# A transformer step on one core: the mixer in two token passes, with the first expert gathers of tile 0 inside it, and GpSimd making one-hot factors

## What is computed

```python
def mixer_and_peer(x, h, o_mla, o_dil, lw):
    y = gate_a * (o_mla @ lw['w_branch_mla']) + gate_b * (o_dil @ lw['w_branch_dil'])  # gates: sigmoid(h @ w_gate)
    x = x + gt1 * (y @ lw['w_out'])
    h2 = modulate(x, lw['norm_ffn_g'], sh2, sc2)          # rms norm, scale, shift
    return x + gt2 * peer(h2, ...)

def peer(hx, w_pq, sub_keys, expert_u, expert_v):
    q = (hx @ w_pq).reshape(n, 8, 2, 128)
    s = einsum('nhpc,hpkc->nhpk', q, sub_keys)            # 8 heads x 2 axes x 128 keys
    top_s, top_i = top_k(s, 16)
    cand = top_s[:, :, 0, :, None] + top_s[:, :, 1, None, :]
    best_s, best = top_k(cand.reshape(n, 8, 256), 16)
    eidx = i1 * 128 + i2                                  # the two keys of each best pair
    g = softmax(best_s)
    a = gelu(einsum('nd,nhkd->nhk', hx, expert_u[eidx])) * g
    return einsum('nhk,nhkd->nd', a, expert_v[eidx])
```

## Time and profile before

| | |
|---|---|
| median of three runs | 4351.54 us (4319.0 to 4370.52) |
| profiled execution | 4370.86 us |
| its span, first to last instruction | 4369.1 us |
| busy: PE, DVE, ACT, POOL | 3802.1, 2723.7, 1199.4, 859.8 us |
| mean granted TensorE clock | 0.913 |

### The profile page before, as it was taken

How to read it: one execution, slowest core, us unless ns; L and a number is a source line. 1 busy time by engine, 2 the same in 40 slices (tenths; PEclk the granted TensorE clock), 3 DMA queues, 4 the chain that set the end, 5 groups by cost and what they waited for, 6 DMA issues and landing times.

```text
span 4369.1 us, 43255 instructions
## 1 busy us (share of the span) xinstructions
PE 3802.1 (87%) x14474; PEld 2490.1 (57%) x14474; DVE 2723.7 (62%) x6374; ACT 1199.4 (27%) x3244; POOL 859.8 (20%) x718
## 2 busy tenths in 40 slices
PE   8798899999981899967997677799999999899896
PEld 7575377888970788953453444344454444445443
DVE  2764562533534111258999987767779676967876
ACT  2564432322332111122222567421111111111111
POOL 0000000001000000003333223333333333344332
PEclk8898998995985899988999888899999999999997
DMA  4001102203116111237888879999999999999997
GB/s 158 7 1 42 29 37 80 81 20 119 51 40 208 55 41 36 100 108 282 323 327 318 314 302 376 399 417 409 410 399 378 414 412 387 384 409 412 387 354 279
DMA packets 255851, 1016.29 MB, mean 233 GB/s; under 512 B 28650, under 2 KB 103810, under 8 KB 170642
## 3 DMA queue, kind: packets, MB, share of 16 engines
q0 software_dynamic: 101520, 723.10, 41.9%
q1 hardware_dynamic: 131218, 280.65, 17.4%
q10 hardware_dynamic: 22896, 9.80, 0.8%
HBM read 964.22 MB, written 49.25 MB: 232 GB/s over the span
## 4 chain that ended last, share of the span: by engine, by line
PE 27%; DVE 15%; DMA 11%; issue 2%; ACT 2%; SPq 0%; POOL 0%; ACTq 0%; DVEq 0%
PE banks L2488 9%; PE banks L2474 9%; DMA ff_room<-in_v 7%; PE banks L2463 4%; DVE ff_rows L2137 4%; PE banks L2411 2%; DVE ff_acc L2103 2%; DMA gates_dram<-ff_room 2%; PE banks L2356 1%; DMA ff_rows<-in_uv,pk_expert 1%; DVE pk_eq L1793 1%; DVE pk_axes L1798 1%; DVE mx_x L2163 1%; PE banks L2435 1%; DVE pk_besti L1772 1%
## 5 line engine op out<-in xcount | busy, mean ns | idle before, releaser
L2035 POOL DMA_INDIRECT ff_rows<-in_uv,pk_expert x640 | 803.0, 1255 | 1519.2 <-DVE ff_acc L2103 831.8
L2137 DVE CUSTOM_DVE_ANT_0 ff_rows<-ff_rows,ff_h_row 128x1024 f32<-128x1024 f32 x648 | 766.6, 1220 | 45.3 <-DMA ff_rows<-in_uv,pk_expert 43.4
L2488 PE MATMUL banks<-ff_room,mx_x 128*128 128x512 f32 x1536 | 702.3, 608 | 57.9 <-DVE mx_x L2178 31.2
L2474 PE MATMUL banks<-mx_x,ff_room 128*128 128x384 f32 x2048 | 685.7, 488 | 12.2 <-ACT mx_x L2321 12.2
L2463 PE MATMUL banks<-ff_rows,o_mla_tops 128*128 128x512 f32 x904 | 446.5, 643 | 144.5 <-ACT o_mla_tops L2231 140.8
L2474 PEld LDWEIGHTS banks<-mx_x,ff_room 128*128 128x128 f32 x2048 | 390.3, 191 | 313.0 <-issue 77.3
L2488 PEld LDWEIGHTS banks<-ff_room,mx_x 128*128 128x128 f32 x1536 | 297.3, 195 | 418.9 <-issue 357.8
L2103 DVE SCALAR_TENSOR_TENSOR ff_acc<-ff_rows,ff_a,ff_acc 128x1024 f32<-128x1024 f32 x388 | 498.6, 1285 | 7.2
L2463 PEld LDWEIGHTS banks<-ff_rows,o_mla_tops 128*128 128x128 f32 x904 | 179.1, 206 | 361.8 <-issue 198.5
L177 PE MATMUL banks<-d_w_high,h_high 128*128 128x512 f32 (+1 forms) x648 | 274.3, 423 | 21.9 <-DVE d_w_low L184 21.0
L2219 ACT ACTIVATE ff_gelu<-ff_dots 128x2 f32<-128x2 f32 x324 | 65.7, 203 | 824.9 <-DVE ff_dots L2137 824.7
(11 more groups left out here) (391 smaller groups left out, 5660.3 us busy)
## 6 DMA issues: line engine op xcount, KB each, us to landing
ff_room<-in_uT SPq DMA_DIRECT2D x128, 512.0 KB, 14.4
ff_room<-in_v SPq DMA_DIRECT2D x128, 512.0 KB, 20.6
gates_dram<-ff_room SPq DMA_DIRECT2D x6, 4096.0 KB, 16.8
mx_x<-gates_dram SPq DMA_DIRECT2D x128, 192.0 KB, 17.2
d_w<-in_w_dil POOLq DMA_DIRECT2D x9, 2048.0 KB, 8.3
d_w<-in_w_ada POOLq DMA_DIRECT2D x32, 512.0 KB, 4.7
ff_room<-in_w_pq SPq DMA_DIRECT2D x32, 512.0 KB, 4.5
ff_rows<-in_uv,pk_expert POOLq DMA_INDIRECT x640, 10.8
```

Of the source, the lines that this page charges most:

```text
L2035: pool.indirect_dma_start(out=rows[r][:, :], out_offset=None, in_=IN["uv"][:, :], in_offset=bass.IndirectOffsetOnAxis(ap=at, axis=0))\
L2137: ins = dve.tensor_tensor_reduce(rows[r][:, 0:D], rows[r][:, 0:D], h_row[i % 2][:], 1.0, 0.0, ALU.mult, ALU.add, dots[:, B % RB, j:j + 1])
L2474: ins = pe.matmul(SD[:, 0:ND], u[e % 4][:, k, :], hd[:, k, :], start=(k == 0), stop=(k == KD - 1))
L2488: ins = pe.matmul(Y[j][:, half], ad[e % 2][:, j * P:(j + 1) * P], v[e % 4][:, half_rows[half]], start=(e == 0), stop=(e == NK - 1))
```

## The change

**stage_mix in two passes.** Pass 0 takes the first 256 tokens (`EARLY` tiles 0 and 1) through gates, output, residual and norm; pass 1 takes the other 776 in two chunks of 388. A unit is now one branch and one gate (`side`), 16 in pass 0 and 32 in pass 1, counted by `u` (by `z` from pass 1's start). All weight tiles are loaded and split twice. After pass 1's second unit (`ROUTER_AT`) come the queries, keys, top 16 and picks of tiles 0 and 1's router that stood in the next stage's prologue. Then 30 of tile 0's 64 batches (`MIX_BATCHES`) run inside pass 1: one per unit from `z` = 5 to 30 but for 16 and 28, then one per second output unit. They have two slots of two rows (`RB` = 2), and DVE does their dot products and their sums.

**stage_ffn.** Tile 0 has 34 batches left, so the dense loop begins at batch 98 instead of 128. `HOT0` is 58, with three quads per batch (`HOTS`), so 32 batches. POOL makes all first factors, behind the gathers of two batches later; ACT makes the second factors of every third quad (`by_act`), DVE those of the other two. There are two `stage` buffers; the second lies in four of the ten row buffers, and so batches 56 to 95 have three slots (`FEW`) instead of five. `ON_VEC` has 10 batches instead of 15. Rows of `h` go to memory from SP.

```diff
+EARLY, MIX_BATCHES = 2, 30
...
+    PASSES = [[(0, NE)], [(NE, NE + CB), (NE + CB, TOK)]]
+    SUBS = [(p, m, side, i) for p in range(2) for m in range(KD) for side in range(2) for i in range(len(PASSES[p]))]
...
+    ROUTER_AT = 1
+    BATCH_AT = [z for z in range(5, 31) if z not in (16, 28)] + list(range(33, 48, 2))
...
+            @block.gpsimd
+            def _(pool):
+                pool.wait_ge(s["half_tile"], 1)
+                for b in range(NB):
+                    for j in range(G):
+                        r = b % RB * G + j
+                        if b >= RB:
+                            pool.wait_ge(s["rsum"], (b - RB) * G + j + 1)
+                        at = c.expert0[:, b * G + j:b * G + j + 1]
+                        pool.indirect_dma_start(out=ring[:, r, :], out_offset=None, in_=IN["uv"][:, :],
...
+                def gated(u):
+                    p, m, side, i = SUBS[u]
+                    c0, c1 = PASSES[p][i]
...
+                    if u >= 3:
+                        pe.wait_ge(s["y"], u - 2)
+                    src = c.o_dilT if side else c.o_mlaT
+                    for k in range(KO):
+                        pe.matmul(out, wb[b % 2][:, side * KO + k, :], src[:, k, c0:c1], start=(k == 0), stop=(k == KO - 1))
+                    pe.wait_ge(s["w_lo"], n + 1)
+                    for k in range(KD):
+                        ins = product3(pe, gate, w_parts(n, k), [t[:, k, c0:c1] for t in h_parts], k == 0, k == KD - 1)
...
+                for u in range(S1, len(SUBS)):
+                    gated(u)
+                    if u == S1 + ROUTER_AT:
...
+                        queries(0)
+                        for hp in range(HP):
+                            if hp + 1 < HP:
+                                queries(hp + 1)
+                            scores(hp)
...
+                def weights(b):
+                    act.wait_ge(s["dot"], b + 1)
+                    act.activation(act_of[:, b % RB], dots[:, b % RB], ACT.Gelu).then_inc(s["gelu"], 1)
...
+                for z in range(len(SUBS) - S1):
+                    sums_due(z)
+                    mixed(S1 + z)
+                    for n in made_after(S1 + z):
+                        w_low(dve, n)
...
+                    if 2 <= z <= 4:
+                        picks(z)
+                    dots_due(z)
...
-    batches = [(i, b) for i in range(NS) for b in range(TAILB if i == TAIL else PER)]
+    batches = [(i, b) for i in range(NS) for b in range(0 if i else MIX_BATCHES, TAILB if i == TAIL else PER)]
...
-    PICK0, HOT0, HOTS = HP * LATE_PER + 3, HP * LATE_PER + 13, 2
+    PICK0, HOT0, HOTS = HP * LATE_PER + 3, HP * LATE_PER + 10, 3
...
+    by_act = lambda q: q % 3 == 1
+    FEW, FEW_AT, MANY_AT = 3, HOT0 - 2, HOT0 + QUADS // HOTS + 6
...
-        stage = part(0, NK * GBLK).rearrange("p (a n) -> p a n", n=GBLK)
+        second = ring[:, FEW * G:FEW * G + 4].rearrange("p r f -> p (r f)")
+        stage = [t.rearrange("p (a n) -> p a n", n=GBLK) for t in (part(0, NK * GBLK), second)]
...
+                    for q in quads_at(B - 2):
+                        pool.wait_ge(s["p_copy"], q // (P // 4) + 1)
+                        if q >= RQ:
+                            pool.wait_ge(s["hot_mm"], q - RQ + 1)
+                        for k in range(4):
+                            at = 4 * q + k
+                            ins = pool.tensor_scalar(hot1[q % RQ][:, k], c.iota[:], pick(0, at), pick(2, at),
+                                                     ALU.is_equal, ALU.mult)
+                        ins.then_inc(s["hot1"], 1)
...
-                        for k in range(4):
-                            at = 4 * q + k
-                            ins = dve.tensor_scalar(hot1[q % RQ][:, k], c.iota[:], pick(0, at), pick(2, at),
-                                                    ALU.is_equal, ALU.mult)
-                        ins.then_inc(s["hot1"], 1)
-                        if q % 2:
-                            continue
...
-                                act.wait_ge(s["g_out"], 16 * (q // BQ))
+                                act.wait_ge(g_out[q // BQ % 2], 16 * (q // BQ // 2))
```

More of the change, by code:

```diff
@@ L11 @@
 import concourse.bass as bass
+import math
 import numpy as np
@@ L1563, in stage_mix @@
         ts = sb("ts", [P, KD, NSA])
[L1564 to L1568, removed]
+        dots, act_of, a = (sb(t, [P, RB, G]) for t in ("dots", "gelu", "a"))
@@ new lines, in stage_mix @@
+        pk = Picks(c, ctx, [0], "px_", [c.expert0], [c.gate0],
+                   [c.x_normed[:, at:at + PH // 2, 0:NE] for at in (0, PH // 2)])
+        acc, h_row = c.acc0, c.o_mlaT[:, :, 0:NE]
+        s = {n: c.sem("mx_" + n) for n in ("w_hi w_lo mm sig y y_hi y_lo out_mm out stored sq sum root inv xn h2 "
+                                           "keys_in q_mm q_copy sc_mm sc_copy top h_mm h_copy half_tile "
+                                           "dot gelu a rsum").split()}
+        gs, sh = c.gs[:, 1], c.mod[:, 3]
@@ L1607, in _, with weight @@
[L1607 to L1610, removed]
+                def weight(n):
+                    before = n - 4 if n < W1 else n - 4 if n < W1 + 2 else n - 2
+                    if before >= 0:
+                        name, value = freed(before)
+                        sp.wait_ge(s[name], value)
+                    p, q = divmod(n, W1)
+                    src = IN["w_gate"][q % 2 * KD + q // 2] if q < 2 * KD else IN["w_out"][q - 2 * KD]
+                    sp.dma_start(w[slot(n)], src).then_inc(w_in[slot(n)], 16)
@@ new lines, in _ @@
+                for n in range(S1, S1 + 4):
+                    weight(n)
+                sp.wait_ge(s["mm"], S1)
+                residual(0)
+                for n in range(S1 + 4, W1):
+                    weight(n)
+                branch(KD)
+                branch(KD + 1)
+                weight(W1)
+                weight(W1 + 1)
+                keep(0)
+                weight(W1 + 2)
+                for n in range(2, HP):
+                    queries(n)
+                weight(W1 + 3)
@@ new lines, in sums @@
+                def sums(b):
+                    dve.wait_ge(s["a"], b + 1)
+                    for j in range(G):
+                        v, weight = ring[:, b % RB * G + j, D:2 * D], a[:, b % RB, j:j + 1]
+                        if b == 0 and j == 0:
+                            ins = dve.tensor_scalar(acc, v, weight, None, ALU.mult)
+                        else:
+                            dve.wait_ge(s["rsum"], b * G + j)
+                            ins = dve.scalar_tensor_tensor(out=acc, in0=v, scalar=weight, in1=acc, op0=ALU.mult, op1=ALU.add)
+                        ins.then_inc(s["rsum"], 1)
@@ new lines, in sums_due, with dots_due @@
+                def sums_due(z):
+                    if z in batch_at and batch_at[z]:
+                        sums(batch_at[z] - 1)
+                def dots_due(z):
+                    if z in batch_at:
+                        dot(batch_at[z])
+                for n in range(3):
+                    w_low(dve, n)
+                for u in range(S1):
+                    mixed(u)
+                    for n in made_after(u):
+                        w_low(dve, n)
+                y_low(0)
+                for m in range(KD):
+                    for n in made_beside(0, m):
+                        w_low(dve, n)
+                    added(m)
```

725 lines of the change are left out of this document (460 added, 265 removed).

## The result

The changed kernel takes 4427.09 us (median of 4 runs, 4415.57 to 4448.88) against 4345.72 for the kernel before (4 runs). The ratio on record, taken over the runs in the fast state, is 1.0169, with a 95% interval of 1.0126 to 1.0211 (the two medians divide to 1.0187). The changed kernel is **slower by 1.7%** where 3% faster was forecast; the interval leaves open whether it is more or less than 2%. The profiled execution took 4427.74 us, 4425.9 of them in the span.

The account below looks back on a forecast made before the run. TensorE was taken to bound mixer and dense loop, VectorE and ScalarE's write waits the hot stretch. Terms 91 - 77 - 19 - 72 - 61 = -138 took the profile from 4371 to 4233, the median from 4352 to 4213 us; range 4140 to 4310.

Parts of the forecast that it names:

- two such passes, 0.41: Hot stretch: GpSimd's first factor taken as two memset-like passes, 0.41 us, so GpSimd sets the pace at 7.7 us a batch.
- bound of four passes, 0.8 us: Hot stretch: upper end for GpSimd's factor, read, compare, multiply and write at memset pace; 12.4 us a batch, 397 us.
- the 34 us for picks and late gathers: Hot stretch: added to 246 us of GpSimd's pace for picks in pieces and gathers that land late.
- the 280: Hot stretch, 32 batches: forecast 280 us, 72 less than before; the forecast case allowed 250 to 310 us.
- Rival C: Hot stretch: GpSimd's factor takes over 0.85 us, making the kernel slower; break-even 0.86 us, 4407 at 1.0; 7%.
- Rival A: Hot stretch: GpSimd's factors and VectorE's dots exclude each other; 10.1 us a batch, stretch 323 us, kernel 4256; 17%.
- Rival B: Mixer's pass 1: gathers set the pace with two slots, 9.3 us a batch, losing 58 us instead of 8; 4263; 13%.
- D: Hot stretch gains nothing, staying at 352 us because slots and picks bind, not the factors; kernel 4285; 6%.
- The mixer (+99 for +91): Mixer: forecast to grow from 436 to 527 us, 91 more, mostly the router of tiles 0 and 1.
- the prologue (-85 for -77): Prologue and batches to 47: 120 + 338 us forecast to become 381, 77 less, with gathers starting at once.
- what the 30 batches cost there (8 forecast): Mixer: VectorE's 7.2 us per unit against TensorE's 6.9 makes 24 units lose 0.3 each, 8 us.
- From batch 48 on I forecast -19: Batches 48 to 57, replacing 48 to 60 ahead of the hot stretch: 94 us forecast to become 75, 19 less.

Follow-up runs that it names:

- experiment 1: The changed kernel with GpSimd's first factors of the hot stretch in eight forms in turn, seven leaving them incomplete: 4328.98 us (one run), hot stretch 322.0.
- experiment 3: The changed kernel with the hot stretch's dot products reading their second input from PSUM, half of `h` twice: 4390.27 us (one run).
- experiment 2: The changed kernel with each GpSimd first factor replaced by a memset of the same tile: 4258.0 us against 4377.22 for the kernel before (one run each).
- experiment 8: The changed kernel with 15 batches of tile 0 in the mixer instead of 30: 4476.63 us (one run).
- experiment 7: The changed kernel with the change from five row slots to three at batch 60 instead of 56: 4413.52 us (one run).
- experiments 5 and 6: The changed kernel with first factors split between GpSimd and VectorE, ScalarE making half the second factors: 4290.07 us; then also three slots from batch 60: 4283.06 us.
- experiment 11: The kernel with split factors and three slots from batch 60, its five slots back at batch 93 instead of 96: 4281.89 us (4 runs).

## Why the prediction was wrong

**The step that failed** is "I take two such passes, 0.41": the factor took 0.78 us undisturbed and 0.95 on the mean (366 us by 384). My own bound of four passes, 0.8 us, was the right number, though not for the right reason: it counts a start of 0.1 us in each pass, where experiment 1 shows one start of 0.35. I took half of it with no row for the choice, and then let the range end at 310 us for the stretch although the bound stood at 397. That bound was not even worked out like the forecast: the 34 us for picks and late gathers stand in the 280 alone, not in the 397 nor in the rivals. With them the bound would have been 431, a loss. In the event they don't come on top: GpSimd is idle 16 of the 433 us, the rest is 352 of factors and 65 of gathers. The experiments share out the 153 us by which 433 exceeds 280: without the turns the stretch takes 386 (experiment 3), so the turns are 47 us and the dearer operation the other 106. The estimate from the Trainium skill (GPSIMD Engine Reference, Performance versus the Vector engine), 0.56 us, was nearer than mine, yet still short: 0.78 against VectorE's 0.28 is 2.8 times, not two (the page's ratio is of an add of two tensors, 2048 columns long).

**Rival C** came true by its condition, over 0.85 us: measured 0.95. Its reason, the operation, makes only 0.78 of that, below its break-even of 0.86; without the turns the kernel took 4390 against 4377 before (experiment 3, one run each), about level. **Rival A** is a true mechanism and it came on top: I had weighed A and C as two cases, but turns lengthen each factor, so they add up. It charged 2.4 us a batch; the 47 us of experiment 3 are 1.5. **Rival B** fell: the units of pass 1 lie 7.2 us apart, as forecast (first dot products of the mixer's batches 0 and 19, 20 units apart, at 1690.0 and 1833.6). **D** fell with experiment 2.

**The other terms.** The mixer (+99 for +91) and the prologue (-85 for -77) hold; the router is one block, 1571.6 to 1639.7, 68 us for the 70 of the earlier trace rows; what the 30 batches cost there (8 forecast) is too small for experiment 8 to measure. From batch 48 on I forecast -19 and got +20. Of these 39 us, 19.5 are my misplaced cut, which the two stretches behind it give back in the sum, and 12 are the step of the slots, which I had costed at nothing (experiment 7). Batches 90 to 97 took 74 instead of 48. Of these 26 us, 10 vanish in experiments 5 and 6. It may be that GpSimd's last factors come earlier there (in the changed kernel the last one starts at 2892.6, 16 us into that stretch), but in experiment 1 they came early too and the stretch took 73, so this is not shown. The rest stays with the last write or the full DMA (experiment 11). The dense loop didn't change, as forecast.

With the measured hot stretch in place of the 280, the other terms as they were, the sum would have been 4371 - 138 + 153 = 4386 for the profile: no longer faster, and with the step of the slots and the longer batches 90 to 97 on the slower side.

## What to carry to other kernels

An operation that a trace doesn't show on an engine gets its dearest bound as the working value when the engine would become the bottleneck; a range that ends short of the bound one has worked out is too narrow. Price a move to an idle engine per instruction, start included (0.35 us of 0.78 here), and ask what its neighbour reads at that moment. An idle engine is worth a share of the work, or none if another has room: with the factors split, or with ScalarE helping instead, the change gained 2%; with all of them on GpSimd it lost 1.7%.

## What the hardware showed beyond that

GpSimd's factor instruction had a start of 0.35 us and 3.35 ns a column; one over 512 columns (2.07) cost less than three over 128 (2.34). A VectorE dot hardly suffers from a factor beside it (median 1.21 us for those that begin beside one, longest 1.53; 1.22 in the earlier trace rows), while the factor grows from 0.78 to 2.80: between these two the turns are one-sided here. VectorE's second factors, with one tensor to read, were longer too: a median of 0.36 us for those that begin beside a factor of GpSimd, 0.29 for the 15 with none beside them; why is not shown. TensorE's granted clock, between its levels of 1.2 and 2.4 GHz, was 0.75 of full speed in the changed hot stretch, where TensorE waits for GpSimd, and 0.91 with memsets in place of factors; its busy time for about as many matmuls (998 and 1019) went from 277 to 222 us. That is not why the stretch is long: TensorE was busy 277 of its 433 us and waited for GpSimd.
